# Second block's norms: modulated features 256 columns wide on ScalarE and VectorE, residual steps ahead of the norms, projection opening with a feature pair

## The chip, the cores and the metric

The kernel runs on one core of a Trainium2 chip. The metric is the device time of one execution in microseconds, median of several runs. Every matrix product is made in split precision: each fp32 operand is written as a high part of type fp32r (a rounded fp32 that TensorE multiplies in one pass) and a low part (the rest), and three matmuls (high by high, low by high, high by low) add up to one product. So every weight that comes from HBM passes through ScalarE (the high part, a copy) and VectorE (the low part, a subtraction) before TensorE can use it, and so does every activation.

## What is computed

Two transformer blocks of two layers each over one sequence of 256 tokens and 1024 features. The first block (attention variants and a convolutional FFN) is untouched. The second block, cut to what matters:

```python
def second_block(x, c, ...):
    for l in range(2):
        mod = (silu(c) @ ada_w[l] + ada_b[l]).reshape(1, 3, 3, 1024)        # shift, scale, gate of 3 sublayers
        y = swiglu(modulate(x, mod[:, 0, 0], mod[:, 0, 1]), ffn_w13[l, 0], ffn_w2[l, 0])
        x = layer_norm(ALPHA * x + 0.5 * (1 + mod[:, 0, 2]) * y, ln_g[l, 0], ln_b[l, 0])
        y = token_mixer(modulate(x, mod[:, 1, 0], mod[:, 1, 1]), w_in[l], w_out[l], ...)
        x = layer_norm(ALPHA * x + (1 + mod[:, 1, 2]) * y, ln_g[l, 1], ln_b[l, 1])
        y = swiglu(modulate(x, mod[:, 2, 0], mod[:, 2, 1]), ffn_w13[l, 1], ffn_w2[l, 1])
        x = layer_norm(ALPHA * x + 0.5 * (1 + mod[:, 2, 2]) * y, ln_g[l, 2], ln_b[l, 2])
    return x

modulate = lambda x, shift, scale: x * (1 + scale) + shift
```

`token_mixer` projects to features (some of them run through a causal convolution of 4 taps and SiLU), to 24 gate values a token and to token-wise values, and mixes them in three ways.

## The kernel before

**Layout.** `x` holds the tokens in two tiles of 128 rows (row 0 and row 1) by 1024 features. For a product it is turned on TensorE into `hT`: 8 feature tiles (k = 0 to 7) of 128 features by 256 tokens, as `hT_hi` and `hT_lo`. The turned values lie in PSUM banks `ps[2:6]`; `ACC` (`ps[4:8]`) holds the four quarters (row, half of the features) of what an FFN or the output projection gives.

**Weights** come in chunks of up to 128 by 2048 fp32 (1 MB) through a ring of three slots: SP loads into `raw` (L525), ScalarE makes `w_hi` (`hi`, L1256), VectorE makes `w_lo` (`lo`, L1719), TensorE multiplies (L665 to L667 for features, L706 to L708 for tokens, L772 to L774 for an FFN's way down). Semaphores order the ring; each engine runs its own stream in program order, so the order of the work is what is written for each engine.

**An entry** is what lies between two sublayers. In each layer of the second block there are three: entry 1 before the first FFN (modulation with `sub` 0), entry 2 before the input projection (`sub` 1), entry 3 before the second FFN (`sub` 2). Before entries 2 and 3, VectorE makes the residual of each quarter (`residual`: times the gate L2191, plus ALPHA times x L2196, statistics L2200), joins a row's statistics (`statistics`, L2217), ScalarE takes the root (`root`, L1521), VectorE the reciprocal (L2222) and the normalised row (`normal_row`, L2227, one instruction of 1024 columns). TensorE turns a row by 8 transposes (`turn_tile`, L686). The gain and shift of the norm are folded into the modulation for the products; x itself gets them from GpSimd by two instructions over 2048 columns (L634), which start when the last feature is there.

**Modulation before** (`hi_mod`, `lo_mod`) goes row by row, in pieces of 128 columns. Row 0: ScalarE computes all 8 features (`hx`, L1503), and after each pair copies it into `hT_hi` (L1509); VectorE subtracts (L2159). Row 1: ScalarE computes the even features and VectorE the odd ones (L2150). In entries 2 and 3, row 0's modulation runs while row 1 is still in its residual; between the rows stand, in entry 1, a weight split `hi_b(1)`; in entry 2, `hi_b` of the second projection chunk, root of row 1 and `gate_copy`; on VectorE, in entry 3, row 0's subtractions before row 1's norm. `gate_on_all` (L752) spreads the next gate over all partitions on TensorE; in entry 2 it runs between the turns of row 0 and of row 1. `gate_copy` (L1515) takes it out of PSUM.

**The projection** (`B_WIN`) runs over 17 chunks. Before: the gates (24 columns, 24 matmuls, a chunk of 192 columns), then seven pairs of feature tiles (48 matmuls each, 2048 columns), a single one, two more pairs, and the token-wise chunks. For each convolved pair ScalarE applies the last tap (L1620), VectorE the three others (six instructions, L2372), ScalarE SiLU (L1604). VectorE's order is: low part of chunk c+1, then the convolution of chunk c (loop at L2360). The last chunk of the ring that is split before the FFN ends (`next_first` on ScalarE, the last `lo` of `ffn` on VectorE) is the first one of the projection.

**The end of a layer** (`last_row`): residual of a row's two halves, statistics, and the norm with gain and shift (L2235, L2239), first all of row 0, then row 1.

## Time and profile before

| | us |
|---|---|
| median of 3 runs | 2053.57 |
| lowest, highest | 2052.53, 2056.17 |
| the profiled execution | 2053.39 |
| its span, first to last instruction | 2051.6 |
| mean granted TensorE clock | 0.963 of full |
| TensorE, VectorE, ScalarE, GpSimd busy | 93%, 67%, 48%, 7% |
| DMA | 374.49 MB, mean 183 GB/s |

The profile is of one execution. Between its span and its time lie 1.8 us of start and end. A line such as L1256 is that of a helper where many places use it. In the timelines each row is an instruction or a run of like ones (x how many); the bracket gives the idle time of the engine before it and what ended that. TensorE's two clock levels are 1.2 GHz (granted 0.50) and 2.4 GHz (1.00).

### The profile page before, as it was taken

What the parts mean: (1) busy time and instruction counts of PE and PEld (TensorE: products, weight loads), DVE (VectorE), ACT (ScalarE), POOL (GpSimd) and SP (SyncE); (2) the same over time, 40 slices, a digit from 0 to 9 for tenths busy, and PEclk for the clock granted to TensorE, in tenths of its full rate; (3) what the DMA queues carried; (4) which work ended last, traced back from release to release, by engine and by line L of the source; (5) the groups of instructions that cost most, each with busy time, mean ns of one, the idle gap of its engine ahead of it and who ended that gap; (6) DMA issues with size and microseconds to landing.
All of it is one profiled execution on the core that took longest, in us unless ns stands there. A gap on an engine that the chain in (4) does not pass through costs nothing. (4 is left out here: it accounts for less than half of the span.)

```text
span 2051.6 us, 32375 instructions
## 1 busy us (share of the span) xinstructions
PE 1912.1 (93%) x12730; PEld 1751.3 (85%) x12730; DVE 1384.0 (67%) x2236; ACT 983.1 (48%) x1579; POOL 152.1 (7%) x204
## 2 busy tenths in 40 slices
PE   6899999889899989998999999997999899989997
PEld 5788999678799979997888889997999788979997
DVE  4476778647677866677666586677666767657445
ACT  5566444555644464445545354445443645434442
POOL 0000000000000000002003220000000200602000
PEclk9999999999999999999899899998999999989999
DMA  6215777421577767763430157765775243025552
GB/s 256 75 63 197 291 268 290 157 74 62 185 288 268 290 225 271 289 242 123 148 110 1 65 221 282 284 253 215 273 285 182 93 136 101 1 103 185 185 185 81
DMA packets 54515, 374.49 MB, mean 183 GB/s; under 512 B 6016, under 2 KB 6656, under 8 KB 12800
## 3 DMA queue, kind: packets, MB, share of 16 engines
q1 hardware_dynamic: 51536, 361.98, 48.6%
q0 software_dynamic: 2304, 9.93, 1.4%
q8 instruction: 79, 1.29, 0.3%
q10 hardware_dynamic: 560, 0.99, 0.2%
q14 instruction: 36, 0.29, 0.0%
HBM read 371.83 MB, written 1.05 MB: 182 GB/s over the span
## 5 line engine op out<-in xcount | busy, mean ns | idle before, releaser
L665 PE MATMUL bank<-hT_hi,w_hi 128*128 128x256 f32 x2432 | 702.1, 289 | 26.1 <-DVE hT_lo L2159 15.3
L666 PE MATMUL bank<-hT_lo,w_hi 128*128 128x256 f32 x2432 | 698.1, 287 | 0.0
L667 PE MATMUL bank<-hT_hi,w_lo 128*128 128x256 f32 x2432 | 697.7, 287 | 0.0
L1719 DVE TENSOR_TENSOR w_lo<-raw,w_hi 128x2048 fp32r<-128x2048 f32 (+2 forms) x270 | 624.7, 2319 | 90.0 <-ACT w_hi L1256 89.9
L1256 ACT ACTIVATE w_hi<-raw 128x2048 fp32r<-128x2048 f32 (+2 forms) x270 | 505.5, 1875 | 163.1 <-PE bank L774 116.2
L665 PEld LDWEIGHTS bank<-hT_hi,w_hi 128*128 128x128 f32 x2432 | 475.3, 195 | 36.1 <-issue 20.8
L666 PEld LDWEIGHTS bank<-hT_lo,w_hi 128*128 128x128 f32 x2432 | 475.3, 195 | 3.2 <-issue 0.5
L667 PEld LDWEIGHTS bank<-hT_hi,w_lo 128*128 128x128 f32 x2432 | 474.7, 195 | 0.7
L772 PE MATMUL bank<-w_hi,hid_hi 128*128 128x512 f32 x528 | 206.7, 391 | 2.1 <-DVE hid_lo L1785 2.1
L773 PE MATMUL bank<-w_lo,hid_hi 128*128 128x512 f32 x528 | 206.2, 391 | 0.0
L774 PE MATMUL bank<-w_hi,hid_lo 128*128 128x512 f32 x528 | 205.4, 389 | 0.0
L1315 ACT ACTIVATE scratch<-bank 128x256 f32<-128x256 f32 x88 | 33.7, 383 | 294.9 <-PE bank L667 294.9
L1713 DVE SCALAR_TENSOR_TENSOR scratch<-scratch 128x1024 f32<-128x1024 f32 x144 | 172.4, 1220 | 0.5 <-DMA scratch<-in_wm 0.5
L1785 DVE TENSOR_TENSOR hid_lo<-scratch,hid_hi 128x256 fp32r<-128x256 f32 x132 | 63.2, 479 | 157.1 <-ACT hid_hi L1321 157.1
L706 PE MATMUL bank<-w_hi,hT_hi 128*128 128x512 f32 (+3 forms) x384 | 152.7, 398 | 15.7 <-DVE w_lo L1719 7.9
L707 PE MATMUL bank<-w_lo,hT_hi 128*128 128x512 f32 (+3 forms) x384 | 149.5, 389 | 0.0
L708 PE MATMUL bank<-w_hi,hT_lo 128*128 128x512 f32 (+3 forms) x384 | 149.0, 388 | 0.0
L772 PEld LDWEIGHTS bank<-w_hi,hid_hi 128*128 128x128 f32 x528 | 99.4, 188 | 22.8 <-DVE hid_lo L1785 3.0
L774 PEld LDWEIGHTS bank<-w_hi,hid_lo 128*128 128x128 f32 x528 | 99.1, 188 | 21.0
L773 PEld LDWEIGHTS bank<-w_lo,hid_hi 128*128 128x128 f32 x528 | 99.4, 188 | 18.2
L1783 DVE TENSOR_TENSOR scratch<-scratch,bank 128x256 f32<-128x256 f32 x132 | 55.2, 418 | 84.7 <-ACT scratch L1315 81.5
L706 PEld LDWEIGHTS bank<-w_hi,hT_hi 128*128 128x128 f32 x384 | 74.8, 195 | 32.1 <-DVE w_lo L1719 14.6
(379 smaller groups left out, 2324.2 us busy)
## 6 DMA issues: line engine op xcount, KB each, us to landing
raw<-in_wb SPq DMA_DIRECT2D x158, 1024.0 KB, 4.9
raw<-in_wa SPq DMA_DIRECT2D x94, 1024.0 KB, 4.9
scratch<-in_wm SPq DMA_DIRECT2D x72, 1024.0 KB, 7.0
raw<-in_wb SPq DMA_DIRECT2D x8, 940.0 KB, 4.7
raw<-in_wb SPq DMA_DIRECT2D x4, 936.0 KB, 4.6
lnw<-in_ln_g POOLq DMA_DIRECT2D x6, 512.0 KB, 4.8
lnw<-in_ln_b POOLq DMA_DIRECT2D x6, 512.0 KB, 5.9
scratch<-in_c SPq DMA_DIRECT2D x5, 512.0 KB, 3.7
```

What stands on the lines that cost most here:

```text
L665: nc.tensor.matmul(out, ah, bh, start=(i == 0), stop=False)
L666: nc.tensor.matmul(out, ah, bl, start=False, stop=False)
L667: last = nc.tensor.matmul(out, al, bh, start=False, stop=(i == n - 1))
L706: nc.tensor.matmul(bank[:, 0:width], hT_hi[:, k, rows], w_hi[:, slot, cols], start=(k == 0), stop=False)
L707: nc.tensor.matmul(bank[:, 0:width], hT_hi[:, k, rows], w_lo[:, slot, cols], start=False, stop=False)
L708: last = nc.tensor.matmul(bank[:, 0:width], hT_lo[:, k, rows], w_hi[:, slot, cols], start=False, stop=(k == KT - 1))
L772: nc.tensor.matmul(out, ah, bh, start=first, stop=False, skip_group_check=True)
L773: nc.tensor.matmul(out, ah, bl, start=False, stop=False, skip_group_check=True)
L774: return nc.tensor.matmul(out, al, bh, start=False, stop=stop, skip_group_check=True)
L1256: nc.scalar.activation(w_hi[:, slot, 0:width], raw[:, raw_slot, 0:width], ACT.Copy).then_inc(hi_done, 1)
L1713: return nc.vector.scalar_tensor_tensor(out=w, in0=w, scalar=1.0, in1=cb, op0=ALU.mult, op1=ALU.mult, accum_out=column)
L1719: nc.vector.tensor_tensor(w_lo[:, slot, 0:width], raw[:, raw_slot, 0:width], w_hi[:, slot, 0:width].bitcast(F32), ALU.subtract).then_inc(l ...
```

## The change

1. **Modulation in features of 256 columns.** Both rows are turned first. `turn_row` fills four banks, each with two features of both rows, and signals each bank when row 1 is turned. ScalarE computes features 0, 1, 4, 5 (`mod_pair`), VectorE 2, 3, 6, 7 (`mod_one`); ScalarE copies into `hT_hi` and VectorE subtracts, in pieces of one, one, two, two and two features (`hi_part`, `lo_part`). Nothing of row 0 is modulated before row 1 is there. In entry 1, `hi_b(1)` goes ahead of the modulation.
2. **All residual steps, then the normalisations.** In entry 2 VectorE makes all four quarters before the first normalised row; in entry 3 it normalises row 1 straight after its statistics; at a layer's end both rows' residuals stand ahead of both `last_row`s. A row is normalised in two halves of 512 columns, each signalled, and TensorE turns the two banks of a half. `gate_on_all(1)` stays between the turns of row 0 and row 1.
3. **The projection opens with a feature pair.** `B_WIN` starts with features 0 and 1, then the gates, then the other pairs. The chunk that is split before the FFN ends is so 2048 columns wide, and the one after it 192.
4. Semaphore counts follow: the root is now signalled apart from the statistics (`ag`).

The core of the diff:

```diff
-B_WIN = ([((), 0, 0)] + [((f, f + 1), 0, 0) for f in range(0, 14, 2)] + [((14,), 0, 0), ((15, 16), 0, 0), ((17, 18), 0, 0)]
+B_WIN = ([((0, 1), 0, 0), ((), 0, 0)] + [((f, f + 1), 0, 0) for f in range(2, 14, 2)] + [((14,), 0, 0), ((15, 16), 0, 0), ((17, 18), 0, 0)]
...
+            def turn_row(i, ready):
+
+                for b, bank in enumerate(TP):
+                    ready(b // 2)
+                    for k in range(2):
+                        cols = slice((2 * b + k) * P, (2 * b + k + 1) * P)
+                        last = nc.tensor.transpose(bank[:, k * SEQ + i * P:k * SEQ + (i + 1) * P], x[:, i, cols], ident)
+                    if i:
+                        last.then_inc(B["tp"], 1)
...
-                pe.wait_ge(B["nx"], due(B, "nx", 1))
-                turn_tile(B, x, 0, 1)
+                turn_normal(0, 0)
                 gate_on_all(1)
-                pe.wait_ge(B["nx"], due(B, "nx", TT))
-                turn_tile(B, x, 1, 1)
+                turn_normal(0, 1)
...
+            def mod_pair(v, sub, b):
+
+                act.wait_ge(B["tp"], due(B, "tp", pairs_before(v, "tp") + b + 1))
+                for k in (2 * b, 2 * b + 1):
+                    nc.scalar.activation(hx[:, k, :], TP[b][:, k % 2 * SEQ:(k % 2 + 1) * SEQ], ACT.Identity,
+                                         scale=modc(sub, 1)[:, k:k + 1], bias=modc(sub, 0)[:, k:k + 1]).then_inc(B["tp_mod0"], 1)
+
+            def hi_part(v, k, n):
+
+                act.wait_ge(B[f"tp_mod{k // 2 % 2}"], modulated(v, k + n - 1))
+                nc.scalar.activation(hT_hi[:, k:k + n, :], hx[:, k:k + n, :], ACT.Copy).then_inc(B["tp_hi"], 1)
+
+            def hi_mods(v, sub):
+
                 act.wait_ge(B["modl"], due(B, "modl", min(sub, 1) + 1))
+                mod_pair(v, sub, 0)
+                hi_part(v, 0, 1)
+                hi_part(v, 1, 1)
+                mod_pair(v, sub, 2)
+                hi_part(v, 2, 2)
+                hi_part(v, 4, 2)
+                hi_part(v, 6, 2)
...
-                hi_mod(0, 0, 0)
                 hi_b(1)
-                hi_mod(0, 0, 1)
+                hi_mods(0, 0)
...
                 root(0, 0)
-                hi_mod(1, 1, 0)
                 hi_b(B_S0["win"] + 1)
                 root(0, 1)
                 gate_copy(1)
-                hi_mod(1, 1, 1)
+                hi_mods(1, 1)
...
+            def lo_mods(v, sub):
+
+                mod_one(v, sub, 2)
+                lo_part(v, 0, 1)
+                mod_one(v, sub, 3)
+                lo_part(v, 1, 1)
+                lo_part(v, 2, 2)
+                mod_one(v, sub, 6)
+                mod_one(v, sub, 7)
+                lo_part(v, 4, 2)
+                lo_part(v, 6, 2)
...
                 def normal_row(sub, i):
 
                     inverse_std(sub, i)
-                    nc.vector.tensor_scalar(x[:, i, :], x[:, i, :], bag[:, i, 0:1], st[:, 10 + i:11 + i],
-                                            ALU.subtract, ALU.mult).then_inc(B["nx"], 1)
+                    for half in range(2):
+                        cols = slice(half * 512, half * 512 + 512)
+                        nc.vector.tensor_scalar(x[:, i, cols], x[:, i, cols], bag[:, i, 0:1], st[:, 10 + i:11 + i],
+                                                ALU.subtract, ALU.mult).then_inc(B["nx"], 1)
...
                 statistics(0)
-                normal_row(0, 0)
                 for half in range(2):
                     from_down(0, 1, half, split + (FFN_N + NEW))
                 statistics(1)
-                lo_mod(1, 1, 0)
+                normal_row(0, 0)
                 normal_row(0, 1)
-                lo_mod(1, 1, 1)
+                lo_mods(1, 1)
...
                 residual(from_bank(1, 1))
                 statistics(1)
-                lo_mod(3, 2, 0)
                 normal_row(1, 1)
-                lo_mod(3, 2, 1)
+                lo_mods(3, 2)
...
                 for i in range(TT):
                     for half in range(2):
                         from_down(2, i, half, split + (B_N + NEW))
+                    statistics(i)
+                for i in range(TT):
                     last_row(2, i)
```

## Rows read from the trace of the kernel before

**Rows 1.** Page, part 1: span; busy time and share, instructions (x) of each engine.

```profile
span 2051.6 us, 32375 instructions
PE 1912.1 (93%) x12730; PEld 1751.3 (85%) x12730; DVE 1384.0 (67%) x2236; ACT 983.1 (48%) x1579; POOL 152.1 (7%) x204
```

**Rows 2.** TensorE's groups by line: busy us, mean ns | idle before them, releasers.

```profile
L665 PE MATMUL bank<-hT_hi,w_hi 128*128 128x256 f32 x2432 | 702.1, 289 | 26.1 <-DVE hT_lo L2159 15.3 <-DVE w_lo L1719 10.2 <-DVE hT_lo L1751 0.4
```

**Rows 3.** Timeline (start, us, instruction [idle, releaser]), ScalarE, entry 1: split between rows.

```profile
742.45 1.89 ACT L1256 ACTIVATE w_hi<-raw 128x2048 fp32r<-128x2048 f32 x1
```

**Rows 4.** Groups by line and shape: xcount | busy us, mean ns.

```profile
L1312 ACT ACTIVATE scratch<-bank,spa 128x256 f32<-128x256 f32 x44 | 24.8, 564 | 102.4 <-PE bank L667 102.4
L1509 ACT ACTIVATE hT_hi<-scratch 128x256 fp32r<-128x256 f32 x48 | 20.0, 417 | 4.0 <-DVE scratch L2150 2.6
...
L2159 DVE TENSOR_TENSOR hT_lo<-scratch,hT_hi 128x256 fp32r<-128x256 f32 x48 | 19.2, 419 | 10.4 <-ACT hT_hi L1509 9.5
L2150 DVE TENSOR_SCALAR scratch<-bank,modl 128x128 f32<-128x128 f32 x24 | 9.2, 405 | 6.5 <-PE bank L686 6.5
L2227 DVE TENSOR_SCALAR x<-x,scratch,st 128x1024 f32<-128x1024 f32 x8 | 6.5, 813 | 0.3
```

**Rows 5.** Timeline, VectorE, entry 2, layer 0.

```profile
930.47 0.69 DVE L2191 TENSOR_TENSOR scratch<-bank,gateb 128x512 f32<-128x512 f32 x1 [2.74 <-PE bank L774]
...
950.53 8.91 DVE L1719 TENSOR_TENSOR w_lo<-raw,w_hi 128x2048 fp32r<-128x2048 f32 x2
959.79 2.69 DVE L2372 SCALAR_TENSOR_TENSOR scratch<-bank,spa,scratch 128x255 f32<-128x255 f32 x6 [0.35 <-ACT scratch L1620]
962.39 3.70 DVE L1719 TENSOR_TENSOR w_lo<-raw,w_hi 128x2048 fp32r<-128x2048 f32 x1
```

**Rows 6.** Stretches after six entries: busy PE, PEld, DVE, ACT, POOL (x), PEclk, DMA, GB/s.

```profile
1402.40:1405.80 3.40, 3.38 (x16) 3.40 (x17) 2.94 (x7) 3.34 (x6) 0.00 (x0) 0.50 0.04 10
...
1850.40:1856.40 6.00, 5.99 (x28) 6.00 (x29) 5.53 (x7) 4.81 (x7) 3.60 (x1) 0.50 0.17 27
sum 26.50, PE 26.23 PEld 24.79 DVE 23.71 ACT 24.94 POOL 8.53; mean PE 4.37 PEld 4.13 DVE 3.95 ACT 4.16 POOL 1.42
```

**Rows 7.** Timeline, TensorE, first matmuls of the third and fourth projection chunks, layer 0.

```profile
959.50 0.39 PE L665 MATMUL bank<-hT_hi,w_hi 128*128 128x256 f32 x1 [0.38 <-DVE w_lo L1719]
...
966.15 0.39 PE L665 MATMUL bank<-hT_hi,w_hi 128*128 128x256 f32 x1 [0.64 <-DVE w_lo L1719]
```

**Rows 8.** Timeline, TensorE, entry 1, layer 0.

```profile
739.26 1.09 PE L686 MATMUL bank<-cst,x 128*128 128x128 f32 x8 [2.50 <-DVE x L1735]
...
745.74 0.55 PE L665 MATMUL bank<-hT_hi,w_hi 128*128 128x256 f32 x1 [5.38 <-DVE hT_lo L2159]
...
753.67 1.88 PE L752 MATMUL bank<-scratch,cst 128*128 128x512 f32 x4
```

**Rows 9.** Timeline, TensorE, entry 1, layer 1: first matmul.

```profile
1402.42 0.55 PE L665 MATMUL bank<-hT_hi,w_hi 128*128 128x256 f32 x1 [3.63 <-DVE hT_lo L2159]
```

**Rows 10.** Timeline, TensorE, entry 2, layer 0.

```profile
937.31 1.88 PE L752 MATMUL bank<-scratch,cst 128*128 128x512 f32 x4
...
944.84 1.97 PE L686 MATMUL bank<-cst,x 128*128 128x128 f32 x8 [5.65 <-DVE x L2227]
...
948.37 0.38 PE L665 MATMUL bank<-hT_hi,w_hi 128*24 128x256 f32 x1 [1.56 <-DVE hT_lo L2159]
```

**Rows 11.** Timeline, VectorE and TensorE, entry 3, layer 0.

```profile
1193.30 0.21 DVE L2217 BATCH_NORM_AGGREGATE scratch<-scratch 128x2 f32<-128x12 f32 x1
...
1198.44 0.55 PE L665 MATMUL bank<-hT_hi,w_hi 128*128 128x256 f32 x1 [1.57 <-DVE hT_lo L2159]
```

**Rows 12.** Timeline, VectorE, entry 1, layer 1: last split of the FFN, first residual step.

```profile
1380.08 2.29 DVE L1719 TENSOR_TENSOR w_lo<-raw,w_hi 128x2048 fp32r<-128x2048 f32 x1
1382.29 0.68 DVE L2191 TENSOR_TENSOR scratch<-bank,gateb 128x512 f32<-128x512 f32 x1
```

**Rows 13.** Timeline, GpSimd, entry 2, layer 0.

```profile
950.77 13.17 POOL L634 TENSOR_TENSOR x<-x,lnw 128x2048 f32<-128x2048 f32 x2 [210.22 <-DVE hT_lo L2159]
```

More of the change, by code:

```diff
@@ L324, in build @@
         carve(6 * SEQ)
-        gdiag, hx, part = carve(KT, P), carve(KT, P), carve(2, 512)
+        gdiag, hx, part = carve(KT, P), carve(KT, SEQ), carve(2, 512)
         bst, bag, bshift = carve(TT, 2, 6), carve(TT, 2), carve(2, KT)
@@ L679, in to_features, with turn_normal @@
                     last.then_inc(N["tp"], 1)
+            def turn_row(i, ready):
[6 more added lines that the diff above has]
+                        last.then_inc(B["tp"], 1)
+            def turn_normal(sub, i):
+                turn_row(i, lambda half: pe.wait_ge(B["nx"], due(B, "nx", 4 * sub + 2 * i + half + 1)))
             def turn_tile(N, src, i, run):
@@ L1092, in _ @@
                             ready = "conv" if ftiles_b[0] in F_CONV else "fm"
-                            pe.wait_ge(B[ready], due(B, ready, c - 2))
+                            pe.wait_ge(B[ready], due(B, ready, feature_chunk(c - 2)))
                         else:
                             pe.wait_ge(B["gcopy"], due(B, "gcopy", 1))
-                    if c == 0:
+                    if not ftiles and not width:
                         cols = [slice(k * GATES, (k + 1) * GATES) for k in range(KT)]
-                        last = products(G[0][0:GATES, 0:SEQ], [((w_hi[:, s_ % RING, cols[k]], w_lo[:, s_ % RING, cols[k]]),
-                                                                (hT_hi[:, k, :], hT_lo[:, k, :])) for k in range(KT)], (B, 1))
+                        last = products(G[c % 2][0:GATES, 0:SEQ], [((w_hi[:, s_ % RING, cols[k]], w_lo[:, s_ % RING, cols[k]]),
+                                                                    (hT_hi[:, k, :], hT_lo[:, k, :])) for k in range(KT)])
                     for k in range(len(ftiles)):
-                        last = feature_tile(G[c % 2][:, k * SEQ:(k + 1) * SEQ], s_ % RING, k, P * len(ftiles))
+                        last = feature_tile(G[c % 2][:, k * SEQ:(k + 1) * SEQ], s_ % RING, k, P * len(ftiles),
+                                            (B, 1) if c == 0 and k == 0 else None)
                     if width:
@@ L1491, in _ @@
             rms_tile(NEXT, 1, 6 * DEPTH + 3, lambda i, half: act.wait_ge(A["x"], summed(DEPTH - 1, i, half)))
-            def hi_mod(v, sub, i):
-                rows = slice(i * P, (i + 1) * P)
-                act.wait_ge(B["modl"], due(B, "modl", min(sub, 1) + 1))
-                for q in range(KT // 2):
-                    for k in (2 * q, 2 * q + 1) if i == 0 else (2 * q,):
-                        act.wait_ge(B["tp"], turned(B, v, i, turn_bank(k, 1)))
-                        if i:
-                            act.wait_ge(B["tp_lo"], split_in(B, v, 0, k))
-                        nc.scalar.activation(hx[:, k, :], turn_at(i, k, 1), ACT.Identity,
-                                             scale=modc(sub, 1)[:, k:k + 1], bias=modc(sub, 0)[:, k:k + 1]).then_inc(B["tp_mod0"], 1)
-                    own, other = modulated(v, i, q)
-                    act.wait_ge(B["tp_mod0"], own)
-                    if i:
-                        act.wait_ge(B["tp_mod1"], other)
-                    nc.scalar.activation(hT_hi[:, 2 * q:2 * q + 2, rows], hx[:, 2 * q:2 * q + 2, :], ACT.Copy).then_inc(B["tp_hi"], 1)
+            def mod_pair(v, sub, b):
[7 more added lines that the diff above has]
+            def hi_mods(v, sub):
+                act.wait_ge(B["modl"], due(B, "modl", min(sub, 1) + 1))
+                mod_pair(v, sub, 0)
[5 more added lines that the diff above has]
+                hi_part(v, 6, 2)
             def gate_copy(sub):
@@ L2263, in _ @@
                 dve.wait_ge(B["modl"], due(B, "modl", 1))
-                for i in range(TT):
-                    lo_mod(0, 0, i)
+                lo_mods(0, 0)
                 gate_diagonal(0)
```

120 lines of the change are left out of this document (54 added, 66 removed).

## The prediction

> **What bounds the kernel now.** I read the page's busy shares first: TensorE is busy 93% of a 2051.6 us span, VectorE 67%, ScalarE 48% [rows 1]. So the time is TensorE's work, plus what it waits, plus what it does at the lower clock. The groups by line say where it waits: before the first matmuls of a matrix that reads hT, 15.3 us on the last step of the modulated features (L2159) and 10.2 us on split weights (L1719) [rows 2]. The change works on the first and touches the second. The six places are the entries into the second block's three sublayers, in two layers: entry 1 (first FFN), entry 2 (input projection), entry 3 (second FFN). The timelines of TensorE, ScalarE and VectorE around one entry of each kind carry the rest; the middle entry of layer 1 repeats that of layer 0.
>
> **How fast the new modulation is.** All of it starts at S, when the first bank (features 0 and 1, both row tiles) is turned. Prices: ScalarE with scale and bias over 256 columns 0.56, its copy over 256 columns 0.42, over 512 some 0.63 (the 2048-wide split of 1.89 less 1536 columns at the slope between the two, 0.82 ns a column); VectorE's scale-and-shift over 128 columns 0.405, so over 256 about 0.54 (128 more at 1.04 ns); its difference over 256 columns 0.42, over 512 about 0.69 [rows 3, 4, 5]. First matmul: two ScalarE steps of which the second is issued 0.5 after the first, the first copy (S+1.0 to S+1.42), the difference (S+1.46 to S+1.88), hand-over 0.15: F = S+2.0. The rest is a ping-pong of the two engines: pairs 2-3 come at S+4.1, 4-5 at S+5.6, 6-7 at S+6.3. VectorE alone has 4x0.54+2x0.42+3x0.69 = 5.1 and two waits. So the last feature is there at S+6.3 (5.7 to 7.0), and a first 48-matmul chunk is held by its features: three gaps of together 1 us, and 30 matmuls left at S+6.3.
>
> **The clock at an entry.** At all six entries the granted clock is 0.50 when matmuls begin, for 3.4 or 6.0 us in the two shown, 26.5 in sum, 4.4 on average [rows 6]. 48 matmuls take 6.0 us at full clock (959.50 to the end before the 0.64 idle) [rows 7] and 0.213 each at half (16 in 3.40) [rows 6], so each us at half costs 0.44. With 4.4 of it from when the features come steadily, the first chunk ends about F+9.0; with the full clock throughout S+6.3+0.15+30x0.12 = S+10.05, which is F+8.0; with the longest low stretch, F+10.1.
>
> **Entry 1.** Layer 0: row 1 is ready for turning at 739.26 as before (the residual and norm ahead of it are not this block's) [rows 8]. Before, ScalarE then still has row 0's modulation, a 1.89 weight split at 742.45 and row 1's [rows 3]; the first matmul comes at 745.74, the chunk ends at 753.67 [rows 8]. After, the weight split goes ahead of the modulation into the wait, S = 739.75, F = 741.8, end 750.8: **-2.9** (-1.8 to -3.9). Layer 1: the final row is ready at 1396.8 (1402.42 less 3.63 idle [rows 9] and 1.97 of turns at half clock, as at 944.84 [rows 10]); the regrouped residual steps and norms hold the same VectorE work without a gap, so row 1 is not earlier, only row 0 later, which nothing waits for. S = 1397.45, F = 1399.5, end 1408.5, against 1402.42 + 5.8 + 0.44x3.4 = 1409.7: **-1.2** (0 to -2.2). The same regrouping at the kernel's end is worth 0: both rows' VectorE work is the same in sum, the second output transfer still starts last.
>
> **Entry 3.** The last statistic is there at 1193.30 [rows 11]. After: root 0.3, reciprocal 0.2, first half of the row 0.55 (the whole takes 0.813 and halving leaves a fixed part twice [rows 4]), two turns 0.3; row 0's modulation no longer stands between. S = 1194.9, F = 1196.9 against 1198.44 [rows 11], end 1205.9 against 1198.44 + 5.8 + 0.44x6.0 = 1206.9 (6.0 is the low stretch of its twin in layer 1 [rows 6]). But the last feature comes at 1201.2, about when it does now, and the weight splits queue behind it. I take **-0.7** each (-1.9 to +0.2), -1.4 for two.
>
> **Entry 2, where I expect the loss.** Four parts.
> (a) The chunk that is split before the FFN ends is now 2048 wide instead of 192. In the trace's FFN-to-FFN seam that work ends just as the residual can begin, at 1382.29 with no idle ahead [rows 12]; I put +0.3 on the start of the residual, now 930.47 [rows 5].
> (b) All four residual steps (2.18 each), then the norms: row 0's first half is ready at 930.8+8.9+0.2+0.55 = 940.5, row 1's at 941.6. TensorE is through with the FFN some 4 us before that and waits. Now it does the gate broadcast in that time, 937.31 to 939.19 [rows 10]; after, turn_normal(0,0) stands ahead of it in TensorE's queue, and behind it row 1's turns, on ScalarE gate_copy and the whole modulation. So broadcast from 941.6: 1.9 at full clock, 3.4 at half. The bound: done 943.5 to 945.0, S = 944.1 to 945.7; after a 4 us idle I take 945.3. F = 947.3 against 948.37 [rows 10], but the last feature at 951.6 against 950.6 (just ahead of L634 [rows 13]).
> (c) The order of chunks. Before: gates (24 short-weight matmuls), then pair 0-1, whose weights VectorE splits without a convolution ahead of them. After: pair 0-1, gates, pair 2-3; and VectorE's order puts lo of pair 2-3 behind the convolution of pair 0-1. From the last feature (T = 951.6): 30 matmuls to T+3.75; ScalarE's taps and VectorE's convolution end 3.7 later, T+7.5 (in the trace 0.87 from tap to convolution, which takes 2.60 to the next step [rows 5]); a split of 2.2 at the earliest T+9.7. The gates cover TensorE only till T+6.5.
> (d) GpSimd's two gain steps start at the last feature. VectorE's split that ran into the first of them took 6.6 (two in 8.91, the first at the usual 2.29 [rows 12]), the one at 962.39 3.70, each ending 2.1 to 2.2 after one of the two GpSimd steps of 13.17 ends; the convolution (one input in PSUM) runs inside the second at 2.69 [rows 5, 13]. Now each step of 6.57 overlaps one 2.2 split. If GpSimd waits in it, as VectorE does, a step alone takes 4.4 and the two end at T+9.1; the split issued at T+7.5 ends T+11.3. If 6.57 is all its own, they end at T+13.3 and the split at T+15.5. I take the first, since one and the same contention then explains both engines' rows.
> The Trainium skill bears this out in "SBUF — State Buffer", section "SBUF: two separate sides": the pair of ports that VectorE and GpSimd share is held exclusively for a whole instruction, by a VectorE instruction with two SBUF inputs too. "GPSIMD Engine Reference", section "3.1 Elementwise", gives 4497 ns for such an addition of 2048 columns; the trace shows only steps near 6.6, with a split inside. By that page the sum is the one I take; by the row alone, the rival below.
> So pair 2-3 starts at T+11.3 = 962.9 against 959.50, after an idle of near 5 us, hence at half clock again: 7.7 for the chunk. The next pair starts at 970.6 against 966.15 [rows 7]: **+4.5** a layer (+1.4 with full clock throughout and S = 944.1; +7.4 with the longest low stretches), +9.0 for two. What follows in the projection runs on this chain (convolution, split, matmul), so I see nothing that gives it back.
>
> **Sum.** -2.9-1.2-1.4+9.0 = +3.5 on the profiled execution's 2053.39, which stands 0.18 under the median of 2053.57: 2057.1, say **2057**.
>
> **Rivals.** *The clock holds* (faster): shorter gaps keep TensorE at full clock at the entries. For it: the idle ahead of the first matmuls at entries 1 and 3, now 5.38, 3.63 and 1.57 [rows 8, 9, 11], shrinks to under 2. Against: all six entries start low. It decides where the first chunk begins at 2.4 GHz: chunks end at S+10.05, -3.9-2.2-3.8, entry 2 still +1.4 each: -7.1, 2046.5. *GpSimd's step is really 6.5*: pair 2-3 at T+15.5, 4.2 a layer more: +11.9, 2065.5. *The gains are hidden*: at entries 1 and 3 the first matmul comes early, but VectorE's splits and the GpSimd lock behind the last feature (which is hardly earlier at entry 3) set the second chunk; some 4 of the 5.5 fall away: 2061.
>
> **Chances.** Forecast 0.60, clock 0.17, long GpSimd step 0.10, hidden gains 0.13. A measurement of this kernel can tell about 0.2%, 4.1 us, from no change. The forecast, +3.5 with its bounds, puts 0.02 faster, 0.33 same, 0.25 slower; the clock 0.12 faster, 0.05 same; the others 0.21 slower, 0.02 same. Sum: 0.14, 0.40, 0.46. The range leaves out the far end of the clock rival and of the GpSimd rival: 2050 to 2065.
>
> **What would show it.** Right: first matmuls near 741.8, 947, 1197; the broadcast at entry 2 behind row 0's turns; TensorE idle 3 to 6 us before pair 2-3 with w_lo as the releaser; GpSimd steps of about 4.4. Wrong: pair 2-3 starting with the gates' end, modulation steps above 0.6, or a granted clock near 1.00 at the entries.

## The result and the profile after

| | before | after |
|---|---|---|
| median, us | 2053.11 (7 runs) | 2061.66 (7 runs) |
| lowest, highest | 2052.53, 2056.17 | 2060.04, 2062.99 |
| the profiled execution | 2053.39 | 2060.31 |

The ratio is 1.0037, with a 95% interval of 1.0025 to 1.0049: slower by 5 to 10 us, 7.6 at the ratio's centre. A later series gave 1.0028 (1.0019 to 1.0038), medians 2060.43 and 2054.97 (x5 below). The forecast was 2057, and +3.5 us on the profiled execution, which took +6.9.

The page of the changed kernel, part 1, answers to [rows 1]:

```profile
span 2058.5 us, 32227 instructions
...
PE 1919.2 (93%) x12730; PEld 1755.1 (85%) x12730; DVE 1376.4 (67%) x2226; ACT 963.4 (47%) x1513; POOL 144.4 (7%) x204
```

VectorE, ScalarE and GpSimd all have less to do, 76 of ScalarE's and VectorE's instructions are gone, and the kernel is slower: as in [rows 1], their busy time is not what counts. TensorE's first matmuls of a matrix that reads hT (part 5, answers to [rows 2]):

```profile
L673 PE MATMUL bank<-hT_hi,w_hi 128*128 128x256 f32 x2432 | 703.9, 289 | 31.3 <-DVE w_lo L1737 17.8
```

The largest wait is no longer for the modulated features but for split weights: 10.2 us of w_lo have become 17.8. (L1737 is the L1719 of before, L673 is L665, L2170 is L2159, L695 is L686, L774 is L752, L2252 is L2227, L642 is L634, L2394 is L2372. In the runs further down the same lines can lie a few numbers further on.)

Entry 1, layer 0, then layer 1, TensorE's timeline (start, us, instruction, idle ahead and its releaser; answers to [rows 8, 9]):

```profile
739.43 1.09 PE L695 MATMUL bank<-cst,x 128*128 128x128 f32 x8 [2.51 <-DVE x L1753]
741.89 0.55 PE L673 MATMUL bank<-hT_hi,w_hi 128*128 128x256 f32 x1 [1.37 <-DVE hT_lo L2170]
...
750.61 1.88 PE L774 MATMUL bank<-scratch,cst 128*128 128x512 f32 x4
```

```profile
1401.18 0.55 PE L673 MATMUL bank<-hT_hi,w_hi 128*128 128x256 f32 x1 [0.75 <-DVE hT_lo L2170]
```

Row 1 is turned at 739.4 as before, the first matmul comes 2.46 later instead of 6.48, and the first chunk ends at 750.61, 3.1 us earlier. Entry 2, layer 0, TensorE, then VectorE and GpSimd (answers to [rows 5, 7, 10, 13]):

```profile
937.35 1.11 PE L695 MATMUL bank<-cst,x 128*128 128x128 f32 x8 [3.85 <-DVE x L2252]
938.29 3.42 PE L774 MATMUL bank<-scratch,cst 128*128 128x512 f32 x4
941.51 1.23 PE L695 MATMUL bank<-cst,x 128*128 128x128 f32 x8
944.18 0.36 PE L673 MATMUL bank<-hT_hi,w_hi 128*128 128x256 f32 x1 [1.43 <-DVE hT_lo L2170]
...
959.95 0.58 PE L673 MATMUL bank<-hT_hi,w_hi 128*128 128x256 f32 x1 [4.96 <-DVE w_lo L1737]
```

```profile
948.25 0.35 DVE L1737 TENSOR_TENSOR w_lo<-raw,w_hi 128x192 fp32r<-128x192 f32 x1
953.15 2.68 DVE L2394 SCALAR_TENSOR_TENSOR scratch<-bank,spa,scratch 128x255 f32<-128x255 f32 x6 [4.55 <-ACT scratch L1639]
955.75 6.35 DVE L1737 TENSOR_TENSOR w_lo<-raw,w_hi 128x2048 fp32r<-128x2048 f32 x2
969.43 2.68 DVE L2394 SCALAR_TENSOR_TENSOR scratch<-bank,spa,scratch 128x255 f32<-128x255 f32 x6 [7.33 <-ACT scratch L1639]
```

```profile
948.49 9.26 POOL L642 TENSOR_TENSOR x<-x,lnw 128x2048 f32<-128x2048 f32 x2 [207.77 <-DVE hT_lo L2170]
```

Read them together. VectorE idles 4.55 us for the taps of pair 0-1 (953.15), convolves, and only then, at 955.75, turns to the split of pair 2-3; GpSimd's second step ends at 957.75, the two splits at 962.1, so the first of them is done at 959.8, and TensorE, through with the gates, has waited 4.96 us for it. The windows behind the stall show at which clock pair 2-3 runs:

```profile
959.95:965.60 5.65, 5.65 (x26) 5.65 (x27) 2.15 (x1) 0.00 (x0) 0.00 (x0) 0.50 0.81 303
...
965.60:975.00 9.40, 9.33 (x75) 8.95 (x74) 5.19 (x10) 3.53 (x5) 0.00 (x0) 0.99 0.10 41
```

The first 26 of pair 2-3's 48 matmuls take 5.65 us at granted 0.50 (1.2 GHz), the others run at 2.4 GHz. Entry 3, layer 0, answers to [rows 11]; the statistic is there at 1196.53:

```profile
1200.27 0.35 PE L673 MATMUL bank<-hT_hi,w_hi 128*128 128x256 f32 x1 [1.35 <-DVE hT_lo L2170]
```

**Where the time went, part by part.** I cut each profile at row 1's turns at entry 1, at the first residual step of each sublayer, and at the projection's last matmuls with gate rows (1020.06 before). "Idle" is the length less TensorE's busy time. "Slow" is TensorE's busy time times the missing share of the clock, summed over windows of half a microsecond: what the low clock adds to the work.

| stretch | length before | after | change | forecast | idle, change | slow, change |
|---|---|---|---|---|---|---|
| block 1 | 739.26 | 739.43 | +0.2 | 0 | +2.7 | -2.9 |
| entry 1 and FFN, layer 0 | 191.21 | 188.26 | -2.9 | -2.9 | -3.8 | +0.2 |
| entry 2 and projection | 89.59 | 92.20 | +2.6 | +4.5 | +3.2 | -1.2 |
| mixer and output projection | 158.90 | 162.54 | **+3.6** | 0 | 0.0 | +3.3 |
| entry 3 and FFN | 203.33 | 201.83 | -1.5 | -0.7 | +0.4 | -3.0 |
| entry 1 and FFN, layer 1 | 204.28 | 202.48 | -1.8 | -1.2 | -3.9 | +1.6 |
| entry 2 and projection | 85.38 | 92.17 | +6.8 | +4.5 | +3.1 | +3.7 |
| mixer and output projection | 158.96 | 160.19 | **+1.2** | 0 | 0.0 | +0.6 |
| entry 3 and FFN | 203.13 | 202.20 | -0.9 | -0.7 | -1.5 | +0.2 |
| end | 17.56 | 17.20 | -0.4 | 0 | -0.4 | 0 |

The six entries gave +2.3 together, forecast +3.5; the other 4.8 us came from the two mixers, where the change touches nothing. Idle and slow are not independent of each other: entry 3 of layer 0 has no slow time in this profile and 5.15 us of idle, in x5, the second profile of the same kernel, 3.28 slow and 3.77 idle, and its length differs by only 0.9 us. A TensorE that is faster reaches the next wait sooner.

### The profile page after: what moved, and what is told of

Read it like the earlier page. It is cut to its first block, busy times and chain, and to the rows that moved or that the text cites. A ratio compares the mean times of both kernels' runs of the same rounds, so it can differ in the third digit from the quotient of the medians.

```text
span 2058.5 us, 32227 instructions
## 1 busy us (share of the span) xinstructions
PE 1919.2 (93%) x12730; PEld 1755.1 (85%) x12730; DVE 1376.4 (67%) x2226; ACT 963.4 (47%) x1513; POOL 144.4 (7%) x204
## 3 DMA queue, kind: packets, MB, share of 16 engines
HBM read 371.83 MB, written 1.05 MB: 181 GB/s over the span
## 4 chain that ended last, share of the span: by engine, by line
PE 78%; DVE 12%; ACT 6%; issue 2%; DMA 1%; SPq 0%; ACTq 0%; DVEq 0%
PE bank L673 14%; PE bank L674 13%; PE bank L675 13%; PE bank L794 5%; PE bank L795 5%; PE bank L796 5%; PE bank L728 4%; DVE w_lo L1737 3%; PE bank L729 3%; PE bank L730 3%; PE bank L1206 2%; PE bank L1197 1%; PE bank L1205 1%; ACT w_hi L1271 1%; DVE scratch L2394 1%
## 5 line engine op out<-in xcount | busy, mean ns | idle before, releaser
L673 PE MATMUL bank<-hT_hi,w_hi 128*128 128x256 f32 x2432 | 703.9, 289 | 31.3 <-DVE w_lo L1737 17.8
L1737 DVE TENSOR_TENSOR w_lo<-raw,w_hi 128x2048 fp32r<-128x2048 f32 (+3 forms) x270 | 616.8, 2289 | 87.7 <-ACT w_hi L1271 87.6
L1271 ACT ACTIVATE w_hi<-raw 128x2048 fp32r<-128x2048 f32 (+3 forms) x270 | 505.6, 1875 | 166.9 <-PE bank L796 112.4
L673 PEld LDWEIGHTS bank<-hT_hi,w_hi 128*128 128x128 f32 x2432 | 475.1, 195 | 43.0 <-DVE w_lo L1737 19.8
L728 PE MATMUL bank<-w_hi,hT_hi 128*128 128x512 f32 (+3 forms) x384 | 151.7, 395 | 16.7 <-DVE w_lo L1737 7.9
```

Source lines behind the costliest of these rows:

```text
L673: nc.tensor.matmul(out, ah, bh, start=(i == 0), stop=False)
L728: nc.tensor.matmul(bank[:, 0:width], hT_hi[:, k, rows], w_hi[:, slot, cols], start=(k == 0), stop=False)
L1271: nc.scalar.activation(w_hi[:, slot, 0:width], raw[:, raw_slot, 0:width], ACT.Copy).then_inc(hi_done, 1)
L1737: nc.vector.tensor_tensor(w_lo[:, slot, 0:width], raw[:, raw_slot, 0:width], w_hi[:, slot, 0:width].bitcast(F32), ALU.subtract).then_inc(l ...
```

## The experiments

There were four series on three chips, and each is timed against runs of the kernel before on its own chip; "us" is the ratio taken on 2053.6. Each edit is against the changed kernel unless it says otherwise. Where a run is set against the changed kernel below, the two ends are those of its two series, +5.8 and +7.6.

| run | median | ratio to before (95%) | us to before |
|---|---|---|---|
| changed kernel, first series | 2061.66 | 1.0037 (1.0025-1.0049) | +7.6 |
| x5 changed kernel again | 2060.43 | 1.0028 (1.0019-1.0038) | +5.8 |
| x3 gain steps cut | 2058.23 | 1.0021 (1.0011-1.0032) | +4.3 |
| x4 filler | 2056.04 | 1.0010 (0.9998-1.0022) | +2.1 |
| x2 broadcast first | 2052.28 | 0.9988 (0.9978-0.9997) | -2.5 |
| x1 gates first | 2049.98 | 0.9974 (0.9963-0.9984) | -5.3 |
| x6 regrouping undone | 2051.74 | 0.9979 (0.9970-0.9988) | -4.3 |
| x7 split early, gain late | 2046.90 | 0.9963 (0.9950-0.9976) | -7.6 |
| x11 modulation only | 2045.38 | 0.9947 (0.9934-0.9961) | -10.9 |
| x9 kernel before with moves | 2044.04 | 0.9942 (0.9928-0.9955) | -11.9 |
| x12 all moves, rows apart | 2037.50 | 0.9905 (0.9890-0.9920) | -19.5 |
| x8 all moves | 2033.46 | 0.9900 (0.9887-0.9913) | -20.5 |
| x10 all moves, gates first | 2031.76 | 0.9876 (0.9861-0.9891) | -25.5 |

**x5: is the mixers' loss the change's?**

> The changed kernel once more, unchanged. Its profile lost 4.8 us in the two token mixers, which the change does not touch and where TensorE's idle time is the same to 0.02 us (9.29 before, 9.29 and 9.31 after): only the stretches at granted clock 0.50 are longer there. Theory (where the low stretches fall in the mixer varies from execution to execution and is not a cost of the change): this profile shows other lengths than 162.54 and 160.19 us for the mixers with idle times within 0.05 us of those, and a median near 2060, within 3 us of 2061.66. Rival (the change brings them): again 162.5 and 160.2, median 2061.7.

The mixers in three profiles; windows: busy PE, PEld, VectorE, ScalarE, GpSimd (x), then TensorE's granted clock. Before:

```profile
1020.06:1178.96 158.90, 149.62 (x955) 136.72 (x954) 96.65 (x228) 68.47 (x162) 39.76 (x78) 0.91 0.19 66
...
1671.95:1830.91 158.96, 149.68 (x955) 136.74 (x954) 97.88 (x229) 68.46 (x162) 39.78 (x78) 0.91 0.20 70
```

After, first profile:

```profile
1019.89:1182.43 162.54, 153.26 (x956) 140.12 (x955) 97.56 (x230) 68.89 (x162) 39.86 (x78) 0.90 0.20 68
...
1678.91:1839.10 160.19, 150.88 (x955) 137.97 (x954) 97.22 (x229) 68.37 (x162) 39.84 (x78) 0.91 0.20 70
```

The same kernel in x5:

```profile
1020.99:1180.32 159.33, 150.04 (x956) 137.11 (x955) 97.90 (x230) 68.89 (x162) 39.88 (x78) 0.91 0.21 70
...
1676.68:1836.49 159.81, 150.50 (x955) 137.66 (x954) 97.39 (x229) 68.36 (x162) 40.07 (x78) 0.91 0.20 69
```

Length less busy is 9.28, 9.28, 9.28, 9.31, 9.29, 9.31: the waits are the same. Only the busy time differs, by up to 3.6 us for the same 955 matmuls, so it is their speed. In all 14 profiles of this study the mixers' idle stays within 9.27 and 9.31 while their length runs from 157.28 to 162.54 (mean of the 22 in other kernels 160.45; the four of the changed kernel 160.47; the two of before 158.93). Over the 28 stretches slow time runs from 10.4 to 15.5 us and busy time follows it; busy less slow stays within 1.1 us. The theory held in the main: in x5 the mixers take only 1.3 us more than before, so at least 3.5 of the first profile's 4.8 us belong to that execution. It is not shown that all of it does: the four mixers with the old modulation (before and x9) average 158.9 us, the 24 with the new one 160.6, with a scatter of 1.4 and 1.0. Two profiles of the old kind are too few to say whether the low stretches in the mixer are longer on average with the change. Without block 1, x5's profile is 2.7 us longer than before's, against forecast +3.5 and +6.7 in the first. The medians still stand 5.5 to 8.5 apart, and two profiles do not say how the clock falls on average; what the low stretches add on average stays open.

**x1: the order of the chunks.**

```diff
-B_WIN = ([((0, 1), 0, 0), ((), 0, 0)] + [((f, f + 1), 0, 0) for f in range(2, 14, 2)] + ...
+B_WIN = ([((), 0, 0)] + [((f, f + 1), 0, 0) for f in range(0, 14, 2)] + ...
```

> The changed kernel with part 3 taken back: the projection opens with the gates again, then pair 0-1, and the short chunk is again the one split before the FFN ends. Modulation and regrouping stay as changed. Theory (the loss at entry 2 is the order of the chunks: after the last feature T the changed kernel has pair 2-3 only at T+11.6 and runs it at half clock): pair 2-3 starts at about T+9.3, without an idle stretch of 5 us ahead of it, pair 4-5 about 4 us earlier after T than now; 4 us a layer, time near 2053.7. Rival (the loss sits in the regrouped norms and the late broadcast, the order costs nothing): within 2 us of the changed kernel's 2061.7.

Windows of entry 2 with the projection, both layers:

```profile
926.37:1012.51 86.14, 75.54 (x520) 65.63 (x519) 66.98 (x100) 49.14 (x66) 14.45 (x5) 0.94 0.35 119
...
1580.43:1667.29 86.86, 76.57 (x519) 66.89 (x518) 66.62 (x99) 49.15 (x66) 14.45 (x5) 0.92 0.33 112
```

86.1 and 86.9 us against 92.2 twice; idle 10.6 and 10.3 against 15.5 and 15.7. Undoing this one part turns +5.8 to +7.6 into -5.3. It costs about 5 us of idle a layer, and 6 of time, where I had expected 4. The convolution of pair 2-3 starts 41.7 after the first residual step in the changed kernel (969.43), 35.9 before and 36.7 and 37.8 here. GpSimd is busy 14.45 instead of 10.56 us for the same steps: its steps and VectorE's splits collide again, as in [rows 13], but at a place where it costs less.

**x2: the gate broadcast.**

```diff
-                turn_normal(0, 0)
                 gate_on_all(1)
+                turn_normal(0, 0)
                 turn_normal(0, 1)
```

> The changed kernel with the gate broadcast of entry 2 ahead of both rows' turns in TensorE's queue, so in the wait for the first normalised row. Theory (the broadcast, 3.4 us at half clock between row 0's and row 1's turns, delays S by what it overhangs): row 1's turns start near 939.2 instead of 941.5 in layer 0, all that follows at entry 2 moves by 2.3, no change of the stall ahead of pair 2-3; 2.3 a layer, time near 2057. Rival (the turns wait for something else, or the earlier start only moves where the clock is low): first matmul less than 1 us earlier, or a time within 2 us of 2061.7.

TensorE, entry 2, layer 0 (the first residual step is at 931.65 here):

```profile
941.30 3.08 PE L695 MATMUL bank<-cst,x 128*128 128x128 f32 x16 [2.13 <-DVE x L2252]
945.13 0.55 PE L673 MATMUL bank<-hT_hi,w_hi 128*128 128x256 f32 x1 [0.75 <-DVE hT_lo L2170]
...
960.89 0.39 PE L673 MATMUL bank<-hT_hi,w_hi 128*128 128x256 f32 x1 [3.21 <-DVE w_lo L1737]
```

First matmul 13.5 after the first residual step (13.2 in layer 1) against 16.5 and 16.6: 3.0 and 3.4, more than the 2.3 expected, since the broadcast took 3.42 at half clock between the rows' turns and takes 1.88 here (937.29), in the wait. It is 8.3 to 10.1 us faster than the changed kernel; of that 6.4 are this shift. The stall ahead of pair 2-3 shrank too, to 3.21 and 4.41 us, where no change was expected.

**x3: GpSimd's share of the stall.**

```diff
-    nc.gpsimd.tensor_tensor(x[:, :, :], x[:, :, :], lnw[:, k, :]..., op)
+    n = 8 if sub == 0 else DM
+    nc.gpsimd.tensor_tensor(x[:, :, 0:n], x[:, :, 0:n], lnw[:, k, 0:n]..., op)
```

> The changed kernel with GpSimd's two steps after entry 2 (gain and shift of the stream, 2048 columns a row pair) cut to 8 columns of each row; the rest of that gain and shift is left out of the computation. Theory (each step of 4.6 us holds VectorE's split of pair 2-3 out; that split, issued at T+7.5, ends T+11.6 instead of T+9.7): pair 2-3 starts at T+9.8, 1.9 us earlier a layer, with 3 us of idle still ahead of it; time near 2057.5. Rival (GpSimd's part is all of the stall): pair 2-3 starts with the gates' end near T+6.5, 5 us a layer, time near 2051. Other rival (no part): pair 2-3 at T+11.6, 2061.7.

VectorE, then TensorE (first residual step at 926.81):

```profile
955.02 4.48 DVE L1738 TENSOR_TENSOR w_lo<-raw,w_hi 128x2048 fp32r<-128x2048 f32 x2
```

```profile
957.36 0.39 PE L674 MATMUL bank<-hT_hi,w_hi 128*128 128x256 f32 x1 [3.10 <-DVE w_lo L1738]
```

Two splits take 4.48 instead of 6.35, and 3.10 us of stall are left of 4.96: GpSimd's share is 1.9 of the 5, as expected. The time fell by 1.5 to 3.3 (4 expected), which is within the noise: the interval of this run overlaps those of both series of the changed kernel. The other 3.1 are VectorE's order.

**x4: does the idle stretch bring the low clock?** 40 matmuls on features that are there go into an unused bank, behind the gates' chunk.

```diff
                         last.then_inc(chunk_mm, 1)
+                    if c == 1:
+                        pe.wait_ge(B["gateb_ev"], due(B, "gateb_ev", 4))
+                        for n in range(40):
+                            nc.tensor.matmul(S[0][:, 0:SEQ], hT_hi[:, n % KT, 0:P], hT_hi[:, n % KT, :], start=True, stop=True)
```

> The changed kernel with 40 more matmuls (128x256, on features that are there, into an unused PSUM bank) on TensorE behind the gates' chunk, in the 5 us in which it now waits for the split of pair 2-3. They add work that nobody uses. Theory (the idle stretch is what takes the clock down for the 6.5 us behind it, which costs 2.9 us): pair 2-3 starts at the same T+11.6 but runs at granted clock 1.00; 2.9 us a layer, time near 2056. Rival (the low stretch comes anyway, somewhere): granted clock still 0.50 behind the stall or a low stretch of the same length a few us later; time within 2 us of 2061.7.

Windows of the filler and of pair 2-3, layer 1:

```profile
1616.69:1622.70 6.01, 6.01 (x49) 5.88 (x50) 2.15 (x1) 0.00 (x0) 0.00 (x0) 1.00 0.83 301
1611.50:1616.69 5.19, 4.95 (x43) 4.75 (x41) 5.16 (x5) 4.08 (x5) 4.38 (x4) 1.00 0.00 0
```

With TensorE kept busy, 49 matmuls take 6.01 us at granted 1.00, where the changed kernel's 26 took 5.65 at 0.50. The time fell by 3.7 to 5.5 us (5.7 expected), though 80 useless matmuls were added. But the rival has a part too: in layer 0 pair 2-3 also ran at 1.00, and a low stretch (946 to 952) came ahead of it, so that "slow" is 8.3 there against 6.3, and 1.8 against 6.1 in layer 1. In this profile entry 2 with the projection gained only in layer 1 (88.45 us against 92.17); in layer 0 it took 92.63 against 92.20. Single runs went from 2051.8 to 2062.4. The profiles of the other runs with the pair first say the same without a filler: of the ten stalls of 3.1 to 5.0 us ahead of pair 2-3, eight had a low stretch right behind them (not x2 in layer 0, 3.21, nor x6 in layer 1, 3.40); of the eight waits of 1 us or less there (x4, x7, x8, x12) none had. So at this place the low clock comes with the long stall in most cases, not in all.

**x6: regrouping undone at entry 2.**

```diff
                 statistics(0)
+                normal_row(0, 0)
                 for half in range(2):
                     from_down(0, 1, half, split + (FFN_N + NEW))
                 statistics(1)
-                normal_row(0, 0)
                 normal_row(0, 1)
```

> The changed kernel with the regrouping at entry 2 taken back: row 0 is normalised straight after its own residual steps, as before the change; both rows are still turned before the modulation, and the gate broadcast stays between the two rows' turns. Theory (regrouping costs at entry 2, since it puts row 0's turns and with them the broadcast 3.5 us later, while row 1 is ready at the same time): row 0's turns and the broadcast are done before row 1 is ready; first matmul 2 us earlier after the first residual step than the 16.5 us it now takes, nothing else changes; 2 us a layer, near 2057.5. Rival (row 1's readiness sets it and the broadcast does not hold it): first matmul within 0.5 us, time within 2 us of 2061.7.

TensorE, layer 0 (first residual step at 929.37):

```profile
935.96 1.88 PE L774 MATMUL bank<-scratch,cst 128*128 128x512 f32 x4
940.96 1.97 PE L695 MATMUL bank<-cst,x 128*128 128x128 f32 x8 [3.12 <-DVE x L2252]
943.67 0.55 PE L673 MATMUL bank<-hT_hi,w_hi 128*128 128x256 f32 x1 [0.75 <-DVE hT_lo L2170]
```

First matmul 14.3 after the first residual step in both layers instead of 16.5 and 16.6: the 2.2 expected. The broadcast runs at 2.4 GHz in the wait, 1.88 instead of 3.42. The time fell by 10.1 to 11.9, where 4 were expected. TensorE's idle time fell by 7.8 to 9.5: besides the shift, the stall ahead of pair 2-3 is 3.64 instead of 4.96, and the chunks before it now run at half clock (940 to 950) and so cover more of it. That half clock also costs; why the time fell by more than the idle time stays open.

**x11: both undone, the modulation alone** (edits of x1 and x6).

> The changed kernel with part 3 and, at entry 2, part 2 taken back: gates first, row 0 normalised straight after its residual. What is left at the entries is part 1, the modulation 256 columns wide after both rows' turns (and the normalisation in halves). Theory (costs of parts 2 and 3 at entry 2 add): 2.2 us a layer faster than x1, near 2045.5. Rival (once the gates open the projection, row 0's place doesn't matter, since the last feature and not the first matmul sets what follows): equal to x1, near 2050.

2045.4 for a forecast 2045.5, and 5.6 below x1 by the ratios (expected 4.4): on top of x1's edit, x6's still brings something, and the rival is out. But the two costs do not add in full. On the changed kernel x1's edit alone brought 11.1 to 12.9 us and x6's alone 10.1 to 11.9; both together brought 16.7 to 18.5. They overlap by about 5 us. What is left of the change, part 1 with the turns of both rows ahead of it, and what part 2 does at entry 3 and at a layer's end, is worth 10.9 us against the kernel before.

**x7: what of VectorE's order?** GpSimd's zeroing of its tiles also moves ahead of the gain steps (left out of the cut).

```diff
-                    lo_b(B_S0["win"] + c + 1)
+                    if c != 1:
+                        lo_b(B_S0["win"] + c + 1)
+                    if c == 0:
+                        lo_b(B_S0["win"] + 2)
...
+                            if sub == 0:
+                                pool.wait_ge(lo_done, l * B_N + S_A + (B_S0["win"] + (4, 5)[k] + NEW))
                             nc.gpsimd.tensor_tensor(x[:, :, :], ...)
```

> The changed kernel with two moves at entry 2: VectorE splits pair 2-3 ahead of the convolution of pair 0-1, in the 4.5 us in which it now waits for the taps; and GpSimd's two gain steps start only when the splits of pair 4-5 and of pair 6-7 are done, instead of at the last feature T. Theory (the stall ahead of pair 2-3 is nothing but the order convolution, locked split, matmul): pair 2-3 starts when the convolution of pair 0-1 ends, at about T+7.6 instead of T+11.6, right after the gates' end at T+6.5, with about 1 us idle; GpSimd's steps cost at most 0.8 us each where they now stand; 3.5 us a layer, near 2054.5. Rival (the deferred steps hold later splits as much as they now hold the first): no gain, 2060 to 2062. Other rival (TensorE's clock falls after the shorter stall all the same): 1 to 2 us a layer.

VectorE, then TensorE, layer 0 (first residual step at 926.83):

```profile
948.73 2.29 DVE L1741 TENSOR_TENSOR w_lo<-raw,w_hi 128x2048 fp32r<-128x2048 f32 x1 [0.84 <-ACT w_hi L1275]
952.44 2.69 DVE L2401 SCALAR_TENSOR_TENSOR scratch<-bank,spa,scratch 128x255 f32<-128x255 f32 x6 [1.42 <-ACT scratch L1643]
```

```profile
955.27 0.36 PE L677 MATMUL bank<-hT_hi,w_hi 128*128 128x256 f32 x1 [0.99 <-DVE scratch L2401]
```

The stall is 0.99 instead of 4.96, and its releaser is now the convolution: the 1 us and the mechanism foretold. Further on two new waits of 0.84 and 1.05 stand beside the deferred GpSimd steps (expected at most 0.8 each). The time fell by 13.4 to 15.2 instead of 7. No run takes the two moves apart.

**x8: all moves.** x7's, the broadcast of x2, and the early split for every feature chunk:

```diff
-                    lo_b(B_S0["win"] + c + 1)
+                    while c_split < c + (2 if c + 2 < len(B_WIN) - N_TOK else 1):
+                        c_split += 1
+                        lo_b(B_S0["win"] + c_split)
```

> The changed kernel with the gate broadcast of entry 2 ahead of both rows' turns, every feature chunk of the projection split one chunk earlier (ahead of the convolution of the chunk that TensorE is at, instead of behind it), and GpSimd's gain steps deferred as in the run beside this. Theory (the waits in the projection are one chain of convolution, split and matmul): 3.2 us a layer from the broadcast, 4 from pair 2-3, and the waits for w_lo further on (1.84 and 2.10 and some of 0.3 to 0.6 each) shrink by 3 together; 10 us a layer, near 2041. Rival (the later waits are for something else that comes with the split, a transfer or the high part on ScalarE): 7 us a layer, near 2047.

```profile
927.52:1005.35 77.83, 72.84 (x518) 65.83 (x517) 65.49 (x101) 47.52 (x66) 10.65 (x5) 0.96 0.42 139
...
1570.51:1649.69 79.18, 73.37 (x518) 66.46 (x517) 65.53 (x101) 47.51 (x66) 10.67 (x5) 0.96 0.41 137
```

The windows of entry 2 with the projection: 77.8 and 79.2 us, idle 5.0 and 5.8 (15.5 and 15.7 in the changed kernel). The two waits for w_lo further on (1.84 and 2.10) are gone as well: they were the same chain. It is 26 to 28 us under the changed kernel, where 20 were expected.

**x9: the same moves on the kernel before** (early split, late gain steps, no broadcast move).

> The kernel before the change with the two moves of x8 that are not the broadcast: every feature chunk split one chunk earlier on VectorE, GpSimd's gain steps deferred. Theory (most of x8's gain over the changed kernel is VectorE's order in the projection and owes nothing to the change): the waits before the third, fourth, 14th-feature and 17th-feature chunks (0.38, 0.64, 1.83, 2.11 us of idle) go, the 7.2 us at the entry stay; 3.5 to 4.5 us a layer, near 2047. Rival (the moves pay only where the projection opens with a feature pair): 2053 to 2055.

```profile
932.49:1012.68 80.19, 72.32 (x519) 65.11 (x518) 62.34 (x101) 52.37 (x77) 10.67 (x5) 0.94 0.39 135
...
1581.58:1661.77 80.19, 72.07 (x519) 64.98 (x518) 62.26 (x101) 52.36 (x77) 10.69 (x5) 0.96 0.36 129
```

2044.0, 11.9 below the kernel before (7 to 9 expected): entry 2 with the projection takes 80.2 us in both layers, against 89.6 and 85.4. More than half of the 20.5 us that x8 has over the kernel before comes from these two moves, VectorE's order and the later gain steps, and owes nothing to the change.

**x10: x8 with the gates first; x12: x8 with x6's edit.** Both were timed on another chip than x8.

> x8 with part 3 taken back: the projection opens with the gates. Theory (once the split of pair 2-3 is early and unlocked, opening with the pair pays, since the gates then cover the convolution; opening with the gates leaves pair 0-1 waiting for its 2.3 us split after the last feature): 1 us a layer slower than x8, near 2035.5. Rival (part 3 costs in itself, by its place and not by VectorE's order): faster than x8, near 2029.

> x8 with the regrouping at entry 2 taken back (row 0 normalised straight after its residual): the broadcast goes first, row 0's turns fall into the wait for row 1. Theory (row 1's second half is ready at the same time within 0.3 us; only the 8 turns of row 0, 1 to 1.5 us at half clock, go out of the path): 0.5 to 1.2 us a layer, near 2031.5. Rival (no difference to x8): 2033.5.

Both of my theories fell.

```profile
947.92 0.58 PE L677 MATMUL bank<-hT_hi,w_hi 128*128 128x256 f32 x1 [0.23 <-DVE w_lo L1740]
```

x10 is not slower than x8, rather faster (intervals 0.9861-0.9891 and 0.9887-0.9913); its idle is 3.8 and 5.3 against 5.0 and 5.8. Pair 0-1 does begin only when its split is done, 2.3 us after the last feature (947.92 after 945.58), but TensorE has the gates' matmuls to do until then, and the wait is 0.23 (0.64 in layer 1). So part 3 brings nothing even where VectorE's order fits it. x12 is no faster than x8, probably a little slower: its first matmul comes 14.3 after the first residual step in both layers, x8's 13.4 and 14.1. With the broadcast out of the way the regrouping is right by 0.2 to 0.9 us; what cost 2.2 us in the changed kernel was the broadcast queued behind row 0's turns, not the regrouping itself.

The cause in one table: TensorE's idle and slow time of one profile each, without block 1.

| kernel | idle | slow | median to before |
|---|---|---|---|
| before | 81.2 | 45.3 | 0 |
| after, x5 | 78.5, 76.8 | 50.9, 49.3 | +7.6, +5.8 |
| x3 | 73.4 | 52.0 | +4.3 |
| x4, with 80 useless matmuls | 68.1 | 46.8 | +2.1 |
| x2 | 67.7 | 53.8 | -2.5 |
| x1 | 67.7 | 52.6 | -5.3 |
| x6 | 69.0 | 51.6 | -4.3 |
| x11 | 64.8 | 49.2 | -10.9 |
| x7 | 69.5 | 47.3 | -7.6 |
| x9 | 71.9 | 41.2 | -11.9 |
| x12 | 59.4 | 46.3 | -19.5 |
| x8 | 56.6 | 43.5 | -20.5 |
| x10 | 54.9 | 47.8 | -25.5 |

In idle time the changed kernel is even 2.8 to 4.4 us better than the kernel before. It loses that to the clock (+5.5, +4.0) and to 3 to 4 us that the windows count as busy at full clock, mostly at entries 1 and 3, where the first chunk's matmuls now run right behind the features; I read these as gaps too short for the view, which no run here shows.

## Why the prediction was nearly right, point by point

- **Speed of the modulation.** The prices held: 0.56 and 0.54 us for scale and shift of 256 columns on ScalarE and VectorE, 0.41 and 0.64 for the copies, 0.42 and 0.69 for the differences. F = S+2.0: at entry 1 the turns begin at 739.43, and the first matmul is at 741.89 (forecast 741.8). Right.
- **Entry 1.** -2.9 and -1.8 for -2.9 and -1.2. Chunk end 750.61 for 750.8. Right.
- **Entry 3.** -1.5 and -0.9 for -0.7 each; first matmul 1.6 us sooner after the residual starts (1.5 forecast). Right; that in layer 0 no low stretch followed at all was not in the sum, and is luck of the one execution: in x5 it did follow, and the gain there is 0.6.
- **Entry 2 (a), (b).** The residual starts straight after the FFN, and the broadcast stands behind row 0's turns as foretold. It began at 938.29, before row 1 could be turned, and took the 3.4 of the upper bound. First matmul 944.18, that is 16.5 after the first residual step, for a forecast 16.5 (947.3 less 930.8). Right.
- **Entry 2 (c), (d).** T = 948.25; pair 2-3 starts at T+11.7, forecast T+11.3, after 4.96 us of idle, forecast "near 5", at half clock as forecast. GpSimd's steps with no split ahead of them take 9.26 for two, 4.6 each (spans on GpSimd are rough; from start to start it is 4.7), forecast 4.4 from the 6.57 of [rows 13] less the split that each had to wait for. The Trainium skill, "GPSIMD Engine Reference", section "3.1 Elementwise", gives 4497 ns for one such step; the trace agrees. The split that VectorE could start at 955.75 ended only 2.1 after GpSimd's step, at 959.8, and in x3, with hardly a GpSimd step, the same two splits take 4.48 instead of 6.35. That fits the Trainium skill, "SBUF — State Buffer", section "SBUF: two separate sides", by which the shared pair of ports is held for a whole instruction. Pair 2-3 took 8.7 and 8.5 us where the forecast had 7.7, so pair 4-5 begins 41.0 and 40.9 after the first residual step instead of 35.7: +5.3 where the forecast had +4.5, from the 7.7 that was too small. By the whole stretch it is +2.6 and +6.8: that their sum, 9.4, comes so near to 9.0 is in part luck of the clock. The layers differ because the kernel before spent 20.5 us at the low clock in this stretch of layer 0 and 6.8 in that of layer 1.
- **The step that failed** is the one that I did not write down: that all outside the entries costs the same in both kernels. In the mixers it was true of the waits, to 0.03 us, and untrue of the clock. They gave +4.8 for a term of 0; in x5 they gave +1.3, so most of the 4.8 belongs to the single execution. A sum against one profile carries that much uncertainty even where each of its terms is right. The medians are another matter: they rose by 5.5 to 8.5, about twice the forecast, while the six entries gave +2.3 and, in x5, +1.8. The rest is not in the idle time; part of it is the low clock, and why there is more of it on average stays open. That 2061.7 lies inside the range 2050 to 2065 owes something to the width of that range.
- **The rivals.** A long GpSimd step is out (4.6). The clock held in places (944 to 954 at entry 2, all of entry 3 in layer 0) and fell elsewhere instead, so that the rival's -7.1 did not come. Hidden gains: no, the gains of entries 1 and 3 arrived in full.
- **What I had not asked** is what each part is worth by itself. The good part (modulation, x11) gives 10.9 us, and two queue orders took 16.7 to 18.5 back. In my sum the good part was 5.5, since I never costed entry 2 with the modulation alone.

## What to carry to other kernels

An engine that stands in wait for one thing while work for the next chunk lies behind it in its queue is the first place to look: moving the split of the next weights ahead of the convolution, with GpSimd's steps out of its way, was worth as much on the kernel before (11.9, x9) as the good part of the change (10.9, x11). Before a step is moved earlier or later in a list, name for each engine what is queued behind it; the broadcast of 1.9 us cost 3 because it was put between two turns. And compare kernels by idle time per stretch before comparing them by length: in the mixers it repeated within 0.05 us while the length varied by 5. It does not repeat so well everywhere: the changed kernel's two profiles have 60.9 us of idle and 8.1 slow in block 1, which nothing here touches, and 58.4 idle and 12.3 slow. So look at both columns.

## What the runs showed that I had not expected

The mixers, the same instructions with the same waits, took 157.3 to 162.5 us in 28 stretches, and all but about 1 us of that goes with the granted clock. And a removed stall was sometimes worth more than its length: x7 had 7 to 9 us less idle time than the changed kernel and took 13 to 15 us less, x11 12 to 14 less and took 17 to 18.5 less; in x1 the difference (9 to 11 idle, 11 to 13 in time) is within the noise. x4 shows one such case, 26 matmuls in 5.65 us behind a 4.96 us wait at 1.2 GHz against 49 in 6.01 at 2.4 GHz without it. It is no rule for a single edit: in x3 4 us of idle gave 1.5 to 3.3.
